# State-space x by tokens, two blocks of x3 turned through DRAM, and the last weight tile in two halves: one change to a two-block Trainium2 kernel

## What is computed

```python
# block 1, layer 0: a state-space mixer
zxbcdt = x @ w_in                       # 2048 -> z 4096, x 4096, B 1024, C 1024, dt 64
xbc = silu(causal_conv(xbc, 4 taps) + conv_b)      # along the tokens
y = ssd_scan(xs, dt, a, B, C) + xs * d  # 8 groups, 8 heads of 64 features each
y = rms(y * silu(z)) * norm_w;  x = layernorm(ALPHA * x + y @ w_out)
# block 1, layer 1: windowed attention with a gate, then layernorm
# block 2: neighbourhood attention, x3 = x2 + o @ w_o,
#          then out = x3 + relu(rms(x3) @ w1)**2 @ w2
```

## Time and profile before

| what | value |
|---|---|
| median of 3 runs | 2069.11 us (2068.75 to 2069.2) |
| the profiled execution | 2068.77 us |
| its span, first to last instruction | 2067.0 us |
| TensorE busy | 2061.2 us (10047 products and transposes) |
| VectorE busy | 1414.0 us |
| ScalarE busy | 1112.0 us |

### The profile page before, as it was taken

The page is one execution under the profiler, slowest core; times in us unless marked ns, Lnnn a source line. Parts: engine busy times, 40 slices in busy tenths (PEclk is TensorE's granted clock), DMA queues, the critical chain, the costliest instruction groups (busy, mean ns, idle before and its releaser), DMA issues.

```text
span 2067.0 us, 26500 instructions
## 1 busy us (share of the span) xinstructions
PE 2061.2 (100%) x10047; PEld 1719.9 (83%) x10047; DVE 1414.0 (68%) x2200; ACT 1112.0 (54%) x1827; POOL 83.9 (4%) x130
## 2 busy tenths in 40 slices
PE   9999999999999999999999999999999999999999
PEld 8888888888888888888888888888888888888887
DVE  7998888888555889965946666555564545655453
ACT  6666667666434555643746666444554334544432
POOL 0111010111001010000100000000000000000000
PEclk9999999999999999999999999999999999999999
DMA  7777777777665679875666666558786666877674
GB/s 280 239 241 227 230 224 230 237 223 239 227 236 173 207 256 282 245 236 173 198 217 211 204 195 190 176 185 244 240 238 214 193 194 206 242 244 243 195 214 132
DMA packets 141551, 453.66 MB, mean 219 GB/s; under 512 B 16416, under 2 KB 35104, under 8 KB 140784
## 3 DMA queue, kind: packets, MB, share of 16 engines
q1 hardware_dynamic: 130896, 412.29, 64.0%
q0 software_dynamic: 10528, 39.67, 6.0%
HBM read 422.48 MB, written 29.43 MB: 219 GB/s over the span
## 4 chain that ended last, share of the span: by engine, by line
PE 99%; ACT 0%; DMA 0%; DVE 0%; issue 0%; SPq 0%; ACTq 0%; DVEq 0%
PE ps L1662 98%; PE ps L1665 1%; DMA xraw<-in_xt 0%; ACT lnt L687 0%; ACT xhl L690 0%; DVE xhl L1006 0%; DVE res L1015 0%; SPq L547 0%; SPq L541 0%; ACTq L266 0%; DVEq L266 0%
## 5 line engine op out<-in xcount | busy, mean ns | idle before, releaser
L1006 DVE TENSOR_TENSOR wlo<-raw,whi 128x1024 fp32r<-128x1024 f32 (+1 forms) x713 | 865.5, 1218 | 554.3 <-ACT whi L690 552.8
L690 ACT ACTIVATE whi<-raw 128x1024 fp32r<-128x1024 f32 (+1 forms) x713 | 753.1, 1058 | 897.0 <-PE ps L1662 886.3
L1662 PE MATMUL ps<-whi,xhl 128*128 128x512 f32 x2624 | 820.2, 391 | 0.6 <-ACT xhl L690 0.5
L1662 PEld LDWEIGHTS ps<-whi,xhl 128*128 128x128 f32 x2624 | 491.4, 188 | 107.1 <-ACT xhl L690 2.3
L1662 PE MATMUL ps<-wlo,xhl 128*128 128x512 f32 x1312 | 507.6, 389 | 0.0
L1662 PEld LDWEIGHTS ps<-wlo,xhl 128*128 128x128 f32 x1312 | 246.4, 188 | 50.1
L1662 PE MATMUL ps<-xhl,whi 128*128 128x512 f32 (+1 forms) x1032 | 251.2, 392 | 0.5 <-DVE xhl L1006 0.5
L1662 PEld LDWEIGHTS ps<-xhl,whi 128*128 128x128 f32 x1032 | 187.8, 189 | 37.2 <-issue 0.8
L1662 PE MATMUL ps<-whi,hhi 128*128 128x512 f32 x512 | 199.2, 389 | 0.0
L1662 PE MATMUL ps<-wlo,hhi 128*128 128x512 f32 x512 | 199.2, 389 | 0.0
L1662 PE MATMUL ps<-whi,hlo 128*128 128x512 f32 x512 | 199.2, 389 | 0.0
(11 more groups left out here) (210 smaller groups left out, 1787.4 us busy)
## 6 DMA issues: line engine op xcount, KB each, us to landing
raw<-in_w SPq DMA_DIRECT2D x256, 512.0 KB, 4.1
raw<-in_w_qkv SPq DMA_DIRECT2D x96, 512.0 KB, 4.3
raw<-in_w_in SPq DMA_DIRECT2D x95, 512.0 KB, 4.2
raw<-in_w_z SPq DMA_DIRECT2D x64, 512.0 KB, 4.1
raw<-in_w_ao SPq DMA_DIRECT2D x64, 512.0 KB, 4.2
raw<-in_w_bi SPq DMA_DIRECT2D x32, 512.0 KB, 3.6
raw<-in_w_gate SPq DMA_DIRECT2D x32, 512.0 KB, 4.9
raw<-in_w_bo SPq DMA_DIRECT2D x32, 512.0 KB, 4.4
```

Source lines behind the costliest of these rows:

```text
L690: return eng.activation(out, x, ACT.Copy, **kw)
L1006: return eng.tensor_tensor(out, x, y, op)
L1662: return eng.matmul(out, x, y, start=start, stop=stop, skip_group_check=True)
```

## The change

Its parts: (1) x of every group becomes a token unit of 8 tiles ahead of the one feature unit (B, C) of 4 tiles; tiles 0 to 11 are interleaved, one of B and C to two of x. The stationary activations of x take every second token. (2) VectorE turns x out of PSUM by squares, GpSimd carries it through DRAM (`raw_way`) into `raw_rows`, and the convolution reads it there in four stretches of 64 tokens, so each tap is one long instruction and one short one for the edges. (3) The scan begins at `ended("x", g) + 12`: at visit 23 for group 0 (22 before) and at the same visits as before for the others. (4) x3's first two blocks are turned by VectorE and DRAM. (5) The last tile's products for the second tokens are made in two halves of 256 columns; the second half goes to a bank of its own, and the store is two DMAs. Two sets of semaphores are merged (`k_*` and `h_*` into `kh_*`). `in_proj` stays for B and C alone: in VectorE its addition comes 2 visits behind the unit's end, its taps 4 and 5, its last step ("made") 7; in ScalarE the copy at 1, the scaled copies at 3, the tanh at 6.

```diff
         if g == 0:
-            woven(a, b)
+            a, b = features("in", g, "w_in"), unit("x", g, "w_x", 8 * g, 16)
+            for j in range(4):
+                slots.extend(a[j:j + 1] + b[2 * j:2 * j + 2])
         else:
-            slots.extend(a + b)
-        slots.extend(c)
+            slots.extend(unit("x", g, "w_x", 8 * g, 16))
+            slots.extend(features("in", g, "w_in"))
         slots.extend(unit("z", g, "w_z", 8 * g, 16))
...
-            if i in (2, 4, 6):
+            if i in (3, 6, 9):
                 for z in orders:
-                    z.append(("x", 2 * i, 4))
+                    z.append(("x", 4 * i // 3, 4))
...
-    return ended("in", ORDER.index((g, "x3")) // 2) + (8 if g else 11)
+    return ended("x", g) + 12
@@ sync_program @@
+            def store_last():
+                for half in range(2):
+                    c = slice(1536 + 256 * half, 1792 + 256 * half)
+                    w.wait_ge(S["w2r"], 16 + half)
+                    eng.dma_start(a["out"][0, :, c].rearrange("(r c) d -> c r d", r=4)[32:64], res[:, 1, c]).then_inc(S["out"], 16)
@@ gpsimd_program @@
+            def x_values(g):
+                w.wait_ge(S["row_turned"], 2 * g + 2)
+                eng.dma_start(raw_way[g, :, :], xs[g % 2][:, :, :].rearrange("p j a -> p (j a)")).then_inc(S["row_stored"], 16)
+                w.wait_ge(S["row_stored"], 16 * (g + 1))
+                w.wait_ge(S["x_conv"], 4 * g)
+                blocks = raw_way[g, :, :].rearrange("(i a) (c x) -> c a i x", i=4, c=4)
+                for c in range(4):
+                    eng.dma_start(raw_rows[32 * c:32 * c + 32, :, :], blocks[c]).then_inc(S["row_loaded"], 16)
...
+            x_values(0)
             w.wait_ge(S["cum_sb"], 1)
...
             for g in range(GROUPS):
                 if g:
+                    x_values(g)
                     w.wait_ge(S["y_ps"], 4 * g)
@@ scalar_program @@
+            def x_values(g):
+                X = xs[g % 2]
+                yield 7
+                w.wait_ge(S["row_loaded"], 64 * (g + 1))
...
+                for j in range(4):
+                    t, shift = taps(4 * g + j)
+                    act(ACT.Identity, X[:, j, :].rearrange("p (i m) -> p i m", i=4), raw_block(j), bias=shift, scale=t[3]).then_inc(S["ev"], 1)
+                yield 4
+                w.wait_ge(S["made"], 6 * g + 2)
+                for j in range(4):
+                    w.wait_ge(S["x_conv"], 4 * g + j + 1)
+                    act(ACT.Tanh, (th if j < 2 else arg)[:, j % 2, :], X[:, j, :]).then_inc(S["tanh"], 1)
...
             def scan(g):
+                w.wait_ge(S["made"], 6 * g + 6)
@@ vector_program @@
+            def x_values(g):
+                u, X = INDEX["x", g], xs[g % 2]
+                yield
+                w.wait_ge(S["z_turned"], g)
+                for t in range(2):
+                    w.wait_ge(S["weights"], END[u, t])
+                    eng.transpose(X[:, :, :].rearrange("p j a -> p (j a)").rearrange("p (c j b t) -> p t j c b", c=4, j=4, t=2)[:, t],
+                                  ps[:, banks(u)[t], :].rearrange("p (j c a) -> p j c a", j=4, c=4)).then_inc(S["row_turned"], 1)
+                yield 7
+                last = {}
+                for s in (1, 2, 3):
+                    for j in range(4):
+                        t, _ = taps(4 * g + j)
+                        z, raw_z = X[:, j, :].rearrange("p (i m) -> p i m", i=4), raw_block(j)
...
+                        stt(z[:, :, s:64], raw_z[:, :, 0:64 - s], t[3 - s], ALU.mult, z[:, :, s:64], ALU.add)
+                        i = stt(z[:, 1:4, 0:s], raw_z[:, 0:3, 64 - s:64], t[3 - s], ALU.mult, z[:, 1:4, 0:s], ALU.add)
...
+                    yield 1 if s < 3 else 2
+                for j in range(4):
+                    w.wait_ge(S["tanh"], 6 * g + j + 3)
+                    stt(X[:, j, :], (th if j < 2 else arg)[:, j % 2, :], 1.0, ALU.add, X[:, j, :], ALU.mult).then_inc(S["made"], 1)
...
             def into_x(n):
...
+                if n < BY_DRAM:
+                    yield
...
+                    eng.transpose(x3_squares[:, :].rearrange("p (c j t b) -> p t j c b", c=4, j=4, t=2),
+                                  res[:, :, c].rearrange("p t (j c a) -> p t j c a", j=4, c=4)).then_inc(S["row_turned"], 1)
+                    yield 6
+                    w.wait_ge(S["row_loaded"], 64 * (GROUPS + n + 1))
...
+                    tt(ALU.mult, x.rearrange("p i (j m) -> p i j m", j=4), x.rearrange("p i (j m) -> p i j m", j=4),
+                       scales.unsqueeze(1).unsqueeze(3).to_broadcast([P, 4, 4, 64])).then_inc(S["x3_scaled"], 1)
+                    yield 2
+                    for t in range(2):
+                        w.wait_ge(S["x3_high"], 4 * n + 2 * t + 2)
+                        tt(ALU.subtract, x3_columns(xlo, n, t), x3_turned_rows(n, t), x3_columns(xhi, n, t).bitcast(F32)).then_inc(S["x3_low"], 2)
+                    return
...
+            def out_last():
+                w.wait_ge(S["weights"], HALF)
+                stt(res[:, 1, 1536:2048], ps[:, banks(INDEX["w2", 7])[1], :], r2[:, 1:2], ALU.mult, res[:, 1, 1536:2048], ALU.add).then_inc(S["w2r"], 1)
+                w.wait_ge(S["w2r"], 16)
+                w.wait_ge(S["weights"], END[INDEX["w2", 7], 1])
+                stt(res[:, 1, 1792:2048], ps[:, 4, 0:256], r2[:, 1:2], ALU.mult, res[:, 1, 1792:2048], ALU.add).then_inc(S["w2r"], 1)
@@ tensor_program @@
-                    q = mul(ps[:, banks(u)[x], :], left[:, k, x * P:x * P + P], right, start=(u, x) not in opened, stop=last)
...
+                    c = slice(0, 512) if p < 10 else slice(0, 256) if p < 13 else slice(256, 512)
...
+                    bank = ps[:, 4, 0:256] if p > 12 else ps[:, banks(u)[x], c]
+                    tokens = left[:, k, :].rearrange("p (q t) -> p t q", t=2)[:, x] if unit.stage == "x" else left[:, k, x * P:x * P + P]
+                    q = mul(bank, tokens, right[:, c], start=(u, x) not in opened or p == 13 and k == unit.nk - 2, stop=last)
...
             def scan(g):
...
-                w.wait_ge(S["made"], made_at(g, "C"))
+                w.wait_ge(S["made"], 6 * g + 2)
...
-            for n in range(4):
+            for n in range(BY_DRAM, 4):
                 side.at(ended("o", n), into_x(n))
```

More of the change, by code:

```diff
@@ L50 @@
 NH, NL = 5, 8
+BY_DRAM = 2
 PAUSES = {("ao", 0, 12): 1, ("ao", 0, 14): 1}
@@ L143, in plan @@
                 for m in range(NH):
-                    visits.append((i + m * t, i + NH + 1 + (t and m > NH - 3), some(t, range(3), m)))
+                    split = t and m == NH - 1 and units[u].stage == "w2"
+                    products = [(a, k, t, 10 + 3 * half + p) for half in range(2) for a, k, _, p in some(t, range(3), m)] if split else some(t, range(3), m)
+                    visits.append((i + m * t, i + NH + 1 + (t and m > NH - 3), products))
             i += NH - 1
@@ L161, in marks @@
             last["end", u, t] = v, m
+            if 10 <= p < 13:
+                last["half"] = v, m
     used, end, count, where = {}, {}, {}, {}
@@ L170, in marks @@
             where[key[1:]] = at[0]
-    return count, used, end, where
+    return count, used, end, where, half
 def feed(slots, visits):
@@ L354, in build @@
         th = rest("th", [P, 2, T])
-        sums = rest("sums", [P, 2, 2, T])
+        raw_rows = rest("raw_rows", [P, 4, 256])
         xc = rest("xc", [P, 2, 512])
@@ L468, in main_and_rest, with taps, raw_block @@
             return ps[:, b:b + 2, 0:T], ps[:, b:b + 2, T:2 * T]
[L470 to L476, removed]
+        def taps(blk):
             return [cwb[:, blk * 4 + k:blk * 4 + k + 1] for k in range(4)], cwb[:, 192 + blk:193 + blk]
-        blocks_of = [ORDER[2 * n:2 * n + 2] for n in range(24)]
+        def raw_block(j):
+            return raw_rows[:, :, 64 * j:64 * j + 64]
         def gate_of(g):
@@ L591, in sync_program @@
             for n in range(4):
-                for t in range(2):
+                for t in range(2 if n < 3 else 1):
                     side.at(ended("w2", 4 + n, t) + (n < 3), store(n, t))
@@ new lines, in in_proj @@
+                w.wait_ge(S["sum"], g + 1)
+                w.wait_ge(S["cb_ps"], g - 1)
+                w.wait_ge(S["cwb"], 1)
+                for b in range(2):
+                    t, shift = taps(32 + 8 * b + g)
+                    act(ACT.Identity, bc[g % 2][:, b, :], sums[:, b, :], bias=shift, scale=t[3]).then_inc(S["ev"], 1)
+                yield 3
+                w.wait_ge(S["made"], 6 * g)
+                for b in range(2):
+                    w.wait_ge(S["conv"], 2 * g + b + 1)
+                    act(ACT.Tanh, th[:, b, :], bc[g % 2][:, b, :]).then_inc(S["tanh"], 1)
@@ L1612, in vector_program @@
             side.at(19, rope_tables())
-            for n in range(24):
-                side.at(ended("in", n), in_proj(n))
             for g in range(GROUPS):
+                side.at(ended("in", g), in_proj(g))
+                side.at(ended("x", g), x_values(g))
```

(6 more changed lines are left out.)

165 lines of the change are left out of this document (96 added, 69 removed).

## The result

The kernel with the change took 2089.19 us (median of 4 runs, 2088.05 to 2090.5) and the kernel before 2069.15 (4 runs, 2068.75 to 2070.45): ratio 1.0096, interval 1.0078 to 1.0113, so about 20 us slower. I had forecast 2071.9 us and a range of 2062.8 to 2078.5. The result lies above both, and above rival B's 2079. The profiled execution took 2088.59 us, with a span of 2086.8 against 2067.0: **+19.8 us** to be found.

A forecast was written before the change was run, and what follows sets the result against it. TensorE was taken as the bound, busy 2061.2 of 2067.0 us. Gains of -6.35 and costs of +9.5 gave +3.1 on the profiled 2068.77, so 2071.9 us, with a range of 2062.8 to 2078.5.

The forecast's parts named there:

- rival B: Scan's wait for B and C: VectorE later still, edges at 0.17 us, 11.3 plus 5 us early, 2079; chance 0.27.
- x by tokens: State-space stage: 64 tiles go from 2.785 to 2.72 us each, -4.2 us.
- I take nothing: x's stationary loads at every second number: hidden beside 227 ns products, 39 ns of cover left, cost 0.
- the far end: x's stationary loads at twice the length: 149 ns more in each of 768 products, 114 us.
- Rival C: x's loads at every second number show: each 10 ns beyond the cover costs 7.7 us, 2079 and up; chance 0.04.
- The groups 2 to 7: TensorE's scan waits for B and C behind VectorE's 16.4 us queue: 6 x 1.1 = +6.6 us (0 to 11.3).
- the short edges: VectorE's 12 short tap instructions per group at 0.105 us each, 1.3 us of its queue.
- Group 1: Raw x third in GpSimd's queue, trips of 10.8 us: 5 us late for ScalarE, 2 for TensorE (0 to 5).
- The start: Tile 1 by tokens wants its low part with its second product: +0.3 us (0 to 1.1).
- Group 0: x's taps move to VectorE's visits 19 to 21, beside time steps and rotary tables: 0.6 us show (0 to 3).
- x3: Two blocks of transposes leave TensorE for VectorE and DRAM: -1.8 us (-1.6 to -1.9).
- the end: Last tile in halves, store issued some 0.2 us earlier and carrying 128 KB: -0.35 us (-0.8 to +0.2).

The follow-up runs named there:

- experiment 7: Kernel with the change, plus scan's first products one visit later, group 1's raw x before group 0's z, x's tokens side by side: 2065.83 us.
- experiment 1: Kernel with the change, x's stationary activations read as 128 neighbouring tokens instead of every second one: 2085.90 us, ratio 1.0082.
- experiment 2: Kernel before, z's stationary activations read at every second token: 2074.15 us, ratio 1.0025.
- experiment 3: Kernel with the change, scan's first products and VectorE's mask on them one visit later: 2075.33 us, ratio 1.0027.
- experiment 8: Kernel with the change, without VectorE's 12 short edge instructions per group: 2077.41 us, ratio 1.0034.
- experiment 4: Kernel with the change, group 1's raw x carried ahead of group 0's z in GpSimd's queue: 2079.56 us, ratio 1.0049.
- experiment 5: Kernel before, with only two x3 blocks turned by VectorE and DRAM and the last weight tile in halves: 2067.05 us, ratio 0.9991.

## Why the prediction was wrong

*The forecast's figure for x by tokens, "I take nothing" for the loads at every second number: wrong.* I had the far end at 149 ns a product and argued that 39 ns of cover were left. The 3136 loads of this form are busy 592.5 us in after and 587.6 in experiment 7; put on the 512 of them that are x's, that is 10 ns each, some 198 ns a load as an estimate. The loads of x alone, from 325 to 350 us of after, have a mean of 196. That is still less than the 227 of a product, and yet each product costs 6 ns more. The cover was the wrong reasoning: the price shows although the load is shorter than the product that it runs beside. The Trainium skill, "Advanced Engine Details and Errata", section "SBUF Cachelines", says that at least two hits on a line of 16 bytes are needed to absorb the access latency, and that following accesses to the same line run at full performance. Every second number of 4 bytes is two on a line, so by it the loads would cost nothing, as I took it. Experiments 1 and 2 measured 5.1 us over the stage, and these decide. Over 64 tiles this turns -4.2 into +1.0. Rival C, at 0.04, named the place, but it too priced only what goes beyond the cover; a load within it was to cost nothing.

*The groups 2 to 7: mechanism right, size small.* I wrote that VectorE's queue takes 16.4 us from a start at -1.37 and TensorE waits 1.1. In the trace the start is at 367.22, that is -1.4, the order is the one that I listed, and the wait is 1.42. The term that was mis-sized is the short edges: 0.105 from independent instructions on 16 numbers, measured 0.137 here. 12 x 0.03 = 0.4 us is the whole difference. The fixed cost per instruction of the Trainium skill, "VectorE: DVE Perf Modes", section "The TRN2 errata — SBUF-src ops pay a fixed extra latency per instruction", put at 0.16 us, would as an estimate have given 1.8; the trace lies between the two. Experiments 3 and 8 each took the waits away completely, one by a later visit and one by a shorter queue.

*Group 1: the step that failed.* "I make that 5 us late for ScalarE and, behind its and VectorE's lead, 2 us for TensorE (0 to 5)". The place and the queue were right. The lateness was not: ScalarE waited 10.3 us for `raw_rows`, and TensorE lost 10.6, twice the upper bound. The lead was sized well: I took 3 us off, and 10.3 - 7.4, some 2.8, came off. The three trips were priced at 3 x 10.8 = 32.4 us and took 121.75 - 89.10 = 32.65, which was luck: the next trip doesn't wait for the loads of the one ahead to land, so the first two took 8.7 and 8.2 us to the next store's issue, and the last, with its store of 9.1 where the earlier trace rows have 4.3, took 121.75 - 105.94 = 15.8. What was missed is when the first trip starts. A lateness of 5 us would need its start at 111.5 + 5 - 32.4 = 84.1, about one visit later than in before, 81.61; it started at 89.10. In VectorE's queue group 0's squares stand behind x's taps (the last ones at 77.68), which I had moved to visits 19 to 21 in the same paragraph; I asked what that costs TensorE in group 0 and not what it does to GpSimd's queue. The rows show this delay of the first trip, but no experiment removed it alone. The second missing term is the clock, 2.7 us of the 10.6. Experiment 4 shows that the wait for `raw_rows` causes all of it: two requests changed places, and all 10.6 us went.

*The start* cost 0.4 by tile 1, predicted 0.3; in the six other traces with tile 1 by tokens it takes 2.80 to 3.93 us, so this hit is no proof. The 0.44 of tile 0 lies within what it does from trace to trace (4.30 to 6.57). *Group 0* showed 0.63 where I had 0.6. *x3* (-1.83) and *the end* (-0.39) came as worked out, and experiment 5 shows that they hold alone, 2.2 us.

*Rival B* named the right place and the right sign. From its 2079 to the profiled 2088.6 the loads add 5.2, groups 0 and 1 add 6.2 (11.2 against its 5) and the start 0.6, and the six waits take back 2.3 (9.0 against 11.3): 9.7. The three misses had the same direction: the loads at nothing, the edges 0.03 us too cheap, and group 1 outside its own bound. Two smaller slips in the prediction decide nothing: by the Trainium skill's formula the gain is 64 x 0.01 = 0.6 us and not 0.7, and the start of VectorE's queue takes 1.10 us for a copy that the row has at 1.06.

## What to carry to other kernels

A layout that is chosen for the reader of a result (every second token, stretches of 64) is paid by each product and each tap; one copy on an engine with room (1.06 us of ScalarE per group) took both away and made the kernel 3.3 us faster. Where a queue does several round trips through DRAM, find out when the first can start, add them up to the one that somebody waits for, and put that one first. When VectorE's work moves, ask whose transfers start behind it. When work moves to just ahead of its reader, what counts is the whole queue between its input and the reader, and the reader can often move instead.

## What the hardware showed that I had not expected

- Stationary factors read at every second fp32 number cost 6 to 7 ns in each product of 512 columns (233 against 227 ns), though the load's recorded duration is well below the product's spacing.
- Behind a wait of 7.4 us TensorE's granted clock was 0.50 for some 5.7 us, and it stood at 1.00 from 143 us on; this added 2.7 us. Where TensorE waited 1.3 to 1.6 us, visits behind the wait are as before in most groups, but visit 80 took 4.43 in experiment 4 (clock 0.62 from 251.5 to 256 us) and 3.87 in experiment 1 (0.76), against 2.89 in after. The wait ahead of it was 1.63 us in experiment 4 and in after alike, and in after the clock stayed at 1.00. What decides in which execution it falls stays open.
- How long GpSimd waits for a store of 512 KB to DRAM differs much. In the ten traces it waits 6.7 to 8.5 us for the 16 stores that it issues straight behind another trip's four loads, and 2.8 to 7.7 for the 216 others, for half of them less than 4.8. The share of the DMA engines alone doesn't tell: it was 0.90 in the 4.3 us of the earlier trace rows, 1.02 in the 6.0 of z's store in after, and 0.94 in the 9.1 of raw x's. No experiment put a pause between the loads and the store.
